# Opening two transformer blocks' norms onto two weight chunks in turn

## The reference

```
# first stack, each layer:
ada = silu(c) @ w_ada[l] + b_ada[l]                  # 6 shift/scale/gate vectors
h = x * (1 + sc1) + sh1
y = mixer(h, w_in, w_o)                              # attention, 16 heads
x = layer_norm(ALPHA * x + (1 + g1) * y, ln_g[l, 0], ln_b[l, 0])
h = x * (1 + sc2) + sh2
x = layer_norm(ALPHA * x + (1 + g2) * swiglu(h), ln_g[l, 1], ln_b[l, 1])
# second stack, each layer, for x and for the context:
x = x + 0.5 * m2 * swiglu(modulate(rms_norm(x, g), m0, m1))
h = modulate(rms_norm(x, g), m3, m4); x = x + m5 * (attention(h @ w_in) @ w_out)
x = x + 0.5 * m8 * swiglu(modulate(rms_norm(x, g), m6, m7))
```

## Time and profile before

| what | us |
|---|---|
| median of 3 runs (lowest to highest) | 2809.44 (2798.35 to 2812.51) |
| profiled execution, its own time | 2804.64 |
| its span in the trace | 2802.8 |
| PE busy | 2585.8 (92%) |
| DVE busy | 1790.7 (64%) |
| ACT busy | 1082.6 (39%) |
| POOL busy | 227.1 (8%) |

### The profile page before, as it was taken

The page is one execution under the profiler, slowest core; times in us unless marked ns, Lnnn a source line. Parts: engine busy times, 40 slices in busy tenths (PEclk is TensorE's granted clock), DMA queues, the critical chain, the costliest instruction groups (busy, mean ns, idle before and its releaser), DMA issues. The chain is left out here.

```text
span 2802.8 us, 40851 instructions
## 1 busy us (share of the span) xinstructions
PE 2585.8 (92%) x15939; PEld 2187.3 (78%) x15939; DVE 1790.7 (64%) x3244; ACT 1082.6 (39%) x2068; POOL 227.1 (8%) x170
## 2 busy tenths in 40 slices
PE   3767998899999899999999999999999999889999
PEld 3747998868888688887766678887788887777999
DVE  6567776647777755644769675654656533678754
ACT  2243543444443333323338333322333322446553
POOL 2000100001000211100000021110111100100110
PEclk8869999968999999999999999999999999999999
DMA  8924775914666144433620324443244433522653
GB/s 296 272 82 137 258 252 165 273 46 149 227 232 204 45 154 146 134 126 102 163 91 2 115 96 148 147 134 113 84 157 150 136 124 118 147 76 89 213 177 124
DMA packets 354873, 413.80 MB, mean 148 GB/s; under 512 B 24737, under 2 KB 291914, under 8 KB 354618
## 3 DMA queue, kind: packets, MB, share of 16 engines
q1 hardware_dynamic: 352496, 404.13, 45.0%
q0 software_dynamic: 832, 4.65, 0.5%
q10 hardware_dynamic: 1354, 2.43, 0.2%
HBM read 409.56 MB, written 5.27 MB: 148 GB/s over the span
## 5 line engine op out<-in xcount | busy, mean ns | idle before, releaser
L683 DVE TENSOR_TENSOR weight_lo<-raw_weights,weight_hi 128x512 fp32r<-128x512 f32 x1024 | 773.5, 763 | 841.2 <-ACT weight_hi L1243 827.9
L1243 ACT ACTIVATE weight_hi<-raw_weights 128x512 fp32r<-128x512 f32 x1024 | 633.7, 629 | 1295.8 <-PE bank L895 1174.1
L895 PE MATMUL bank<-H_hi,weight_hi 128*128 128x256 f32 (+1 forms) x2832 | 966.8, 341 | 87.5 <-POOL H_lo L853 51.5
L895 PE MATMUL bank<-H_lo,weight_hi 128*128 128x256 f32 (+1 forms) x2832 | 946.4, 334 | 0.0
L895 PE MATMUL bank<-H_hi,weight_lo 128*128 128x256 f32 (+1 forms) x2832 | 945.7, 334 | 0.0
L895 PEld LDWEIGHTS bank<-H_hi,weight_hi 128*128 128x128 f32 x2832 | 547.3, 193 | 182.5 <-issue 96.1
L895 PEld LDWEIGHTS bank<-H_hi,weight_lo 128*128 128x128 f32 x2832 | 547.6, 193 | 50.8
L895 PEld LDWEIGHTS bank<-H_lo,weight_hi 128*128 128x128 f32 x2832 | 548.3, 194 | 47.7 <-issue 1.0
L1546 DVE SCALAR_TENSOR_TENSOR ada_partial<-raw_weights,silu_c,ada_partial 128x512 f32<-128x512 f32 x616 | 442.4, 745 | 1.3 <-DVE ada_partial L1546 0.2
L895 PE MATMUL bank<-hidden_hi,weight_hi 128*128 128x256 f32 (+1 forms) x1056 | 358.9, 340 | 4.7 <-DVE weight_lo L683 4.2
L895 PE MATMUL bank<-hidden_lo,weight_hi 128*128 128x256 f32 (+1 forms) x1056 | 354.9, 336 | 0.0
(11 more groups left out here) (173 smaller groups left out, 2087.1 us busy)
## 6 DMA issues: line engine op xcount, KB each, us to landing
raw_weights<-in_w_ada_dram SPq DMA_DIRECT2D x120, 1024.0 KB, 5.4
raw_weights<-in_w_ffn_up_dram SPq DMA_DIRECT2D x88, 1024.0 KB, 5.7
raw_weights<-in_w_ffn_in_dram SPq DMA_DIRECT2D x44, 1024.0 KB, 5.9
raw_weights<-in_w_ffn_down_dram SPq DMA_DIRECT2D x32, 1024.0 KB, 5.2
raw_weights<-in_w_in_dram SPq DMA_DIRECT2D x18, 1024.0 KB, 5.6
raw_weights<-in_w_ffn_out_dram SPq DMA_DIRECT2D x16, 1024.0 KB, 7.9
raw_weights<-in_w_in_ab_dram SPq DMA_DIRECT2D x12, 1024.0 KB, 8.9
raw_weights<-in_w_in_cd_dram SPq DMA_DIRECT2D x12, 1024.0 KB, 7.9
```

Of the source, the lines that this page charges most:

```text
L683: eng.tensor_tensor(WL[:, p.g % SPLIT, 0:p.kt * CW].rearrange("p (t n) -> p t n", n=CW), raw_ap(ch.n, ch.kt, CW)[:, p.k0:p.k0 + p.kt, :], ...
L895: return pe.matmul(o, w, x, start=start, stop=stop, skip_group_check=True)
L1243: act.activation(WH[:, p.g % SPLIT, 0:p.kt * CW].rearrange("p (t n) -> p t n", n=CW), raw_ap(ch.n, ch.kt, CW)[:, p.k0:p.k0 + p.kt, :], ACT ...
```

## The change

- Behind each of the ten norms, two chunks (`lead`: the gate and up chunks of an FFN's first step, or the first two items of QKV) are used in turn. The order of their eight pieces is one[0], two[0], one[1], two[1], one[2], one[3], two[2], two[3]: both chunks for K tiles 0 to 3, then the first is ended, then the second. PE waits for both bank pairs before it. The splits of the later four pieces stand inside the norm, behind tiles 3 to 6, on ScalarE and on VectorE.
- GpSimd's `low` is gone. ScalarE writes H_hi itself. VectorE writes H_lo: in an RMS norm one scalar_tensor_tensor makes the scaled tile and one H_lo, per 256 columns; at a LayerNorm with a product, a tensor_scalar and a subtraction. The new x of a LayerNorm is written by ScalarE. The tmp tiles are cut so that there are four.
- `busy(n)` behind the sums grows from 22 to 34 (rms) and from 12 to 20 (ln).
- Opening: four loads (three condition rows and the identity) have a semaphore of their own; silu follows them. The other parameters are converted after the third modulation chunk, the lambda work after the mod norm. x is loaded after silu and turned after the seventh chunk; the context is loaded during the first attention and turned in the last LayerNorm.
- na_skew is issued only when the first QKV stage has ended. The first QKV stage hosts 8 modulation chunks instead of 10, the second 9 instead of 7, never behind the first item.
- In the QKV stages of the second stack PE also waits for the squares of items two back.

```diff
-                host = ada_chunk() if len(st.items) < hosted else None
+                host = ada_chunk() if 0 < len(st.items) <= hosted else None
...
-         (2816, ("v", 768))], T, 10, T, 0)
+         (2816, ("v", 768))], T, 8, T, 0)
...
-         (2560, ("v", 512)), (2816, ("v", 768))], T, 8, T, 1)
+         (2560, ("v", 512)), (2816, ("v", 768))], T, 10, T, 1)
...
+    for s, after in zip(PLAN, PLAN[1:]):
+        if after.kind in ("ffn_in", "qkv") and s.kind in ("mod", "ln", "rms"):
+            s.lead = (after.steps[0].g, after.steps[0].u) if after.kind == "ffn_in" else \
+                (after.items[0].chunk, after.items[1].chunk)
+            one, two = (ch.pieces for ch in s.lead)
+            s.lead_order = [one[0], two[0], one[1], two[1], one[2], one[3], two[2], two[3]]
+            PIECES[one[0].g:one[0].g + 8] = s.lead_order
+            after.lead_order = s.lead_order
+    for k, p in enumerate(PIECES):
+        p.g = k
+    def lead_split(s, t, split_next):
+        if s.lead and t >= 3 and t < 7:
+            split_next(s.lead_order[t - 3])
...
+                    pool.wait_ge(ev_act.sem, s.q_in)
+                    for q in range(2):
+                        pool.dma_start(X[:, 4 * q:4 * q + 4, T:2 * T],
+                                       a["ctx_2"][0, P * q:P * q + P, :].rearrange("p (t n) -> p t n", t=4)
+                                       ).then_inc(ctx_in, 16)
...
+            def first(at, ready):
+                st = s.steps[at.u]
                 wait_bank(at, lambda k: s.steps[k].gg)
-                features(at, lambda k: s.steps[k].g, s.steps[at.u].gg, KC, 0, HH, HL, s.n, ready=ready)
+                wait_bank(at, lambda k: s.steps[k].ug)
+                for p in s.lead_order:
+                    if p.chunk is st.g:
+                        features(at, lambda k: s.steps[k].g, st.gg, KC, 0, HH, HL, s.n, ready=ready, only=p.k0 // PIECE)
+                    else:
+                        features(at, lambda k: s.steps[k].u, st.ug, KC, 0, HH, HL, s.n, only=p.k0 // PIECE)
...
-            busy(22 if s.kind == "rms" else 12)
+            if s.last_ln:
+                context()
+            busy(34 if s.kind == "rms" else 20)
...
+            cond = [(ROWS[0][0:8, :], a["c"].rearrange("a (t p) -> (a t) p", p=P)),
+                    (ROWS[0][8:16, :], a["c_2"].rearrange("a (t p) -> (a t) p", p=P)),
+                    (ROWS[0][16:24, :], a["c_ctx_2"].rearrange("(t p) -> t p", p=P)), (ident[:, :], c["ident"])]
+            for dst, src in cond:
+                act.dma_start(dst, src).then_inc(cond_in, 16)
...
+            act.dma_start(XIN[:, :, :], a["x"].rearrange("a (q p) d -> p (a q) d", p=P)).then_inc(tokens_in, 16)
...
+            for t in range(NT):
+                src = NORM_TILE[t % 4] if s.kind == "rms" else NORM_HALF[t % 4]
                 if s.kind != "mod":
...
-                wait_apart(act, h_ready.sem, at(lambda k: s.h + k - 1), act_waited)
+                    act.wait_ge(mod_src.sem, s.src + t + 1)
                 for v in range(s.n // T):
...
+                    cols, sh = slice(v * T, v * T + T), ad[:, 8 * s.shift + t, v:v + 1]
+                    if s.kind == "rms":
+                        ins = act.activation(HH[:, t, cols], src[:, cols], ACT.Identity, bias=sh)
+                    elif s.kind == "ln":
+                        ins = act.activation(HH[:, t, cols], src[:, cols], ACT.Identity, bias=GS[:, t, 1:2],
+                                             scale=GS[:, t, 0:1])
+                    else:
+                        ins = act.activation(HH[:, t, cols], X[:, t, cols], ACT.Identity, bias=sh,
+                                             scale=ad[:, 8 * s.scale + t, v:v + 1])
+                ins.then_inc(mod_hi.sem, 1)
+                if s.kind == "ln":
+                    act.activation(X[:, t, 0:T], src[:, 0:T], ACT.Identity,
+                                   bias=G_COLS[:, s.gain_b + t:s.gain_b + t + 1],
+                                   scale=G_COLS[:, s.gain + t:s.gain + t + 1]).then_inc(x_norm.sem, 1)
+                lead_split(s, t, lambda p: ahead(one, lambda _: p, split, late))
...
+        def lead_rest(s, host):
+            for i, p in enumerate(s.lead_order[4:8]):
+                ahead(one, lambda _: p, split, late)
+                if host:
+                    ada(one, lambda _: host, i, 4)
...
+            def scaled_tile(t):
+                if rms:
+                    if t >= 4:
+                        dve.wait_ge(h_ready.sem, s.h + t - 3)
+                    for v in range(n // T):
+                        cols = slice(v * T, v * T + T)
+                        ins = dve.scalar_tensor_tensor(out=NORM_TILE[t % 4][:, cols], in0=X[:, t, cols],
+                                                       scalar=GS[:, t, v:v + 1], in1=RB[:, cols], op0=ALU.mult,
+                                                       op1=ALU.mult)
+                    ins.then_inc(mod_src.sem, 1)
+                elif s.kind == "ln":
+                    x = NORM_HALF[t % 4][:, :]
+                    if t >= 4 and not s.last_ln:
+                        dve.wait_ge(x_norm.sem, s.xn + t - 3)
+                    ins = dve.tensor_tensor(x, X[:, t, 0:n], RB[:, 0:n], ALU.mult)
                     if not s.last_ln:
...
                         ins.then_inc(mod_src.sem, 1)
                     else:
                         chain.link(ins)
...
+                        chain.mark(dve.tensor_scalar(X[:, t, 0:n], x, G_COLS[:, s.gain + t:s.gain + t + 1],
+                                                     G_COLS[:, s.gain_b + t:s.gain_b + t + 1], ALU.mult, ALU.add))
+            def low_tile(t):
+                if rms:
+                    dve.wait_ge(mod_hi.sem, s.hi + t + 1)
+                    for v in range(n // T):
+                        cols = slice(v * T, v * T + T)
+                        ins = dve.scalar_tensor_tensor(out=HL[:, t, cols], in0=NORM_TILE[t % 4][:, cols],
+                                                       scalar=ad[:, 8 * s.shift + t, v:v + 1],
+                                                       in1=HH[:, t, cols].bitcast(F32), op0=ALU.add, op1=ALU.subtract)
+                else:
+                    full = FULL_HALF[t % 4][:, :]
+                    if s.kind == "ln":
+                        dve.wait_ge(mod_src.sem, s.src + t + 1)
+                        x, sc, sh = NORM_HALF[t % 4][:, :], GS[:, t, 0:1], GS[:, t, 1:2]
+                    else:
+                        x, sc, sh = X[:, t, 0:n], ad[:, 8 * s.scale + t, :], ad[:, 8 * s.shift + t, :]
+                    if t >= 4:
+                        dve.wait_ge(h_ready.sem, s.h + t - 3)
+                    chain.link(dve.tensor_scalar(full, x, sc, sh, ALU.mult, ALU.add))
+                    dve.wait_ge(mod_hi.sem, s.hi + t + 1)
+                    ins = dve.tensor_tensor(HL[:, t, 0:n], full, HH[:, t, 0:n].bitcast(F32), ALU.subtract)
+                ins.then_inc(h_ready.sem, 1)
...
+            for t in range(NT + 1):
+                if t < NT:
+                    scaled_tile(t)
+                if t and not s.last_ln:
+                    low_tile(t - 1)
+                    lead_split(s, t - 1, lambda p: ahead(one, lambda _: p, split, late))
```

225 lines of the change are left out of this document (120 added, 105 removed).

## The result

The changed kernel takes 2757.66 us (median of four runs, 2750.40 to 2771.49) where the kernel before, timed beside it, takes 2803.89 us (2794.31 to 2812.51). The ratio is 0.9846, with a 95% interval of 0.9821 to 0.9872: 1.5% faster. The forecast of 2734 us had the direction, and the range of 2708 to 2765 holds the time; of the gain of 70 to 75 us, 46 came. The profiled executions stand at 2804.64 and 2754.09 us.

The account below looks back on a forecast made before the run. TensorE (92% busy) was taken as the bound, DMA in the first QKV stage. Gains of 8.5 + 17 + 15.2 + 6.5 + 28.2 - 0.4 = 75.0 us gave 2729.6, plus 4.8 for the median: 2734 us (2708 to 2765).

Parts of the forecast that it names:

- Opening: Start of the kernel, up to the first product: waiting for four loads only brings that product 8.5 us earlier (3 to 9.5).
- First QKV stage: First product to first scores: the na_skew copy and two modulation chunks leave, 17.5 us less DMA time; gain 17 us (6 to 24).
- DMA keeps the bound and nearly all of it is won: Step for the first QKV stage: 84 of 101.6 us remain, above 69.1 us of products, so 17 us are gained.
- LayerNorms before the FFNs: Two LayerNorms: shorter tiles and two chunks at once, both done 15.5 us after the reciprocal's end; gain 15.2 us (8 to 17).
- Second QKV: LayerNorm and QKV stage of the second layer: faster norm, but three more modulation chunks to load; gain 6.5 us (-2 to 12).
- the count of 64 us of transfers: Second QKV stage: 10 weight chunks, 8 modulation chunks and 1.1 MB of bias take 64 us of DMA, landing near 556.
- Five wide norms: Five RMS norms at 512 columns: the pair of chunks takes 21.8 instead of 27.42 us; gain 28.2 us (18 to 32).
- Last RMS norm: The 256-column RMS norm: 24 more unread matmuls push the first product by 2.77 us; loss 0.4 us.
- What costs nothing: Side changes taken as free: GpSimd's lost subtraction, modulation group closed after its output projection, context transposes, added QKV wait.
- the ring of four buffers sets it: Rival: norms gain as summed, but both QKV stages keep their pace, 17 and 6.5 falling to 6 and -2; 2754 us, chance 0.17.
- The clock rival: PE's clock falls in pauses of tiles 4 to 7 and at stage heads, about 2.5 us each; 2759 us, chance 0.12.
- The slower rival: In ten norms, ScalarE and DVE wait for a piece PE must free while PE awaits their tile; 2834 us, chance 0.03.

## Why the forecast was right, and where it was not

**Opening (8.5; 9.3 and 10.2).** Right, by the mechanism given: DVE's sums start at 10.36 us (10 forecast) and end at 39.0 (39.5).

**First QKV stage (17; 5.3 and 6.7).** The step that failed is "DMA keeps the bound and nearly all of it is won". Its price of the copy was good, 8.5 to 10.9 us for 10.8; the two chunks are worth 3.0 to 5.4 of the 6.7 forecast. But the step read the share of 0.90 in the middle of the stage and took the saved transfer time off the end. A stage bound by bytes is shortened only if its transfers also start in time. They start when SP's queue passes the bias load, and this is a row that stood in the list of the kernel before, for the other QKV stage. I applied it there and not here, since the opening, slower then, hid it here. From the gate to the scores the stage takes 84.1 us instead of 96.1, so 12.0 of the 14.2 us are won that the copy and the one modulation chunk loaded less behind the gate were priced at; but the gate comes 12.2 us after the first product instead of 5.5, and that takes 6.7 away.

**LayerNorms before the FFNs (15.2; 10.8 and 10.2).** The mechanism is right to a tenth. The forecast had both chunks done at 15.5 us after the reciprocal's end, which is R + 17.25; the 96th product comes at R + 17.18. At that point 8.2 and 7.5 us are won. The term failed behind it: 1.5 and 3.4 us are given back in the FFN's first steps. In the second of them PE has five waits for weight_lo of 0.6 to 1.3 us, 3.8 in all, between R + 24 and R + 60, where the kernel before has two, 0.95 in all. The sum stopped at the 96th product. It also has a slip: the mean of 8.2 and 0.7 less is 7.85, not 7.6. Why these splits come late wasn't tested; that the next chunk is asked for only when a buffer comes free, while PE is further on, is my reading.

**Second QKV (6.5; -3.5 and -3.4).** The step that failed is the count of 64 us of transfers, set against the measured end of before. The transfers start with SP's gate, at R + 13.6 instead of R + 16.7, a gain of 3.1 us, not of the 6.5 that the norm has won at the 96th product (R + 17.2 instead of R + 23.7). From the gate to the scores the stage takes 86.9 instead of 80.3 us. Three modulation chunks more are asked for in that time, as the forecast had it, at a price of 10.1 us. But its count left out what the output projection has loaded in the same time, and was not made for the kernel before. Made there (10 + 5 chunks and 1.1 MB, 54 us) it ends near 554 us, where 570.8 was measured, so it didn't describe this stage. Two like counts would have given 3.1 - 10.1 = -7.0. With as many hosted chunks as before, in the run that puts two back, the stage takes 97.8 us against 97.1 and 96.8: the faster norm alone brought this stage nothing that can be measured. By its own figures the term also has a slip: 570.8 - 563 is 7.8, not 6.5.

**Five wide norms (28.2; 23.5 and 23.3).** Right: 5.8 to 5.9 in the FFN norms (5.6 forecast), 4.8 in the first QKV (5.4), and 1.2 or 5.6 in the second by the clock of the execution. The clock at the heads is part of it: PE arrives warm, as forecast.

**Last RMS norm (-0.4; -2.2 and -1.1).** The products ran through as forecast, in 11.50 us. The unread matmuls moved the first product from R + 3.9 to R + 7.6 in the first profile, where the 68 took 8.63 us, and to R + 6.4 or R + 6.7 in seven others with as many: the sum's 2.77 us was right, and the first profile unlucky. In the second profile the 96th product comes when it did before (R + 17.9 against R + 17.8); the 1.1 us go behind it.

**What costs nothing.** This is the other step that failed. For the first projection it named only DVE's two small operations of the closing; PE's part, 2.46 us before the mean, it didn't name. For the last it said nothing at all. The turn changes what the *preceding* stage must have split, and so loaded, before it can end: 3.9 to 5.3 us lost in the last projection; in the first, where 1.6 to 4.0 were lost, 1.7 by its rows.

**Rivals.** Two gave better numbers than the forecast's 2734. The first, "the ring of four buffers sets it", at 2754 us, had the effect, but its cause only in part: SP's queue more than the ring. The clock rival, at 2759, came nearest, by luck: the clock is 1.00 through the tiles of the LayerNorm and at the heads of the wide norms, where it was to fall, and costs 4.4 us in the last QKV stage in some executions. The slower rival, a lead split that blocks the norm, didn't come: in the wide norms DVE's waits for weight_hi between tiles are 0.4 us.

## What to carry to other kernels

When a stage is bound by transfers, find the event that lets its first transfer go, and move that, before counting bytes off its end. An in-order DMA queue hides its gate as long as something ahead of it is slow; speed that up and the gate shows. When pieces of two loads are interleaved, ask also who must split or load them: the stage before now needs both loads, and a ring has to have room for both. And repeat a profile of both kernels before a stage's difference is believed: here one stage of one kernel moved by 9 us from one execution to the next.

## What the runs showed of the hardware that I had not expected

A pause of TensorE of 1.99 us, after more than ten microseconds of work at 1.00, was followed by ten microseconds at half clock in three profiles, and by the full clock in seven others with the same pause (five of the changed kernel's family, two of the kernel before); the two variants that edit the stage lie between. A pause of 2.25 or 2.76 us before a wide norm's first product was followed by five microseconds at 0.66 to 0.71 in nine of fifteen cases, and at 1.00 in the others. In the attention of the second layer the mean clock of the same instructions lay between 0.50 and 0.94, worth up to 16 us of 2750. A 3.67 MB copy costs about the same, 8.5 to 11 us, at either place where transfers bound the work, and less than 1.5 us beside attention (57.0 to 58.0 us with it, 56.8 to 57.4 without).
